# Third attention of a fused two-block transformer kernel: values in fp32r once a head and branch, a second transposed part, and the normalising pass on GpSimd

## The reference, cut to what matters

```python
o_c = jnp.einsum('bqghk,bkgd->bqghd', p_c, v_cmp)      # compressed keys, 31 of them
...
p_s = masked_softmax(ss, ...)                           # "selected" branch
o_s = jnp.einsum('bghqk,bgqkd->bqghd', p_s.astype(vs.dtype), vs)
...
p_w = masked_softmax(sw, mask_w)                        # "window" branch
o_w = jnp.einsum('bghqk,bkgd->bqghd', p_w.astype(vw.dtype), vw)
out = gc[..., 0:1] * o_c + gc[..., 1:2] * o_s + gc[..., 2:3] * o_w
```

## Time and profile before

| | |
|---|---|
| median of 3 runs | 1900.53 us (1900.32 to 1901.03) |
| the profiled execution: its own time, its span | 1901.72 us, 1899.9 us |
| mean granted clock of TensorE | 0.996 |
| TensorE busy | 1880.1 us (99% of the span) |
| VectorE, ScalarE, GpSimd busy | 879.0, 795.7, 952.2 us |
| nsa attention, first early-gate product to first merge product | 1277.47 to 1394.17 us |

### The profile page before, as it was taken

The page is one execution under the profiler, slowest core; times in us unless marked ns, Lnnn a source line. Parts: engine busy times, 40 slices in busy tenths (PEclk is TensorE's granted clock), DMA queues, the critical chain, the costliest instruction groups (busy, mean ns, idle before and its releaser), DMA issues.

```text
span 1899.9 us, 26936 instructions
## 1 busy us (share of the span) xinstructions
PE 1880.1 (99%) x9217; PEld 1572.9 (83%) x9217; DVE 879.0 (46%) x1814; ACT 795.7 (42%) x1412; POOL 952.2 (50%) x1236
## 2 busy tenths in 40 slices
PE   8999999999999999999999999999999999999999
PEld 6878888888888888888888888888888888888887
DVE  6867642222236675422222673696643354444200
ACT  6558742223233576422232353637652333323221
POOL 6640255554556642555555564552145555555553
PEclk9999999999999999999999999999999999999999
DMA  6330133232332212333323322221123323232332
GB/s 221 101 116 2 40 92 102 95 100 95 94 98 89 83 41 68 97 101 97 100 92 97 99 86 92 67 78 46 34 64 96 97 87 101 93 104 90 111 100 78
DMA packets 47438, 168.30 MB, mean 89 GB/s; under 512 B 5616, under 2 KB 5872, under 8 KB 47088
## 3 DMA queue, kind: packets, MB, share of 16 engines
q1 hardware_dynamic: 46368, 164.64, 27.0%
q10 hardware_dynamic: 976, 2.39, 0.5%
HBM read 164.13 MB, written 2.10 MB: 87 GB/s over the span
## 4 chain that ended last, share of the span: by engine, by line
PE 67%; POOL 14%; issue 14%; DVE 3%; ACT 1%; DMA 0%; POOLq 0%; SPq 0%; ACTq 0%; DVEq 0%
PE bank L611 19%; PE bank L613 19%; PE bank L612 19%; POOL WL L568 14%; PE bank L727 4%; PE bank L695 3%; PE bank L712 2%; PE bank L772 0%; DMA X<-x 0%; PE bank L777 0%; DVE KT L1436 0%; PE bank L666 0%; PE bank L724 0%; ACT PROB L1054 0%; DVE XL L1421 0%
## 5 line engine op out<-in xcount | busy, mean ns | idle before, releaser
L568 POOL TENSOR_TENSOR WL<-RAW,WH 128x256 fp32r<-128x256 f32 x1208 | 934.6, 806 | 919.1 <-ACT WH L990 918.8
L611 PE MATMUL bank<-XH,WH 128*128 128x512 f32 x1311 | 523.3, 399 | 2.0 <-DVE KMV L1758 1.0
L613 PE MATMUL bank<-XH,WL 128*128 128x512 f32 x1311 | 511.5, 390 | 0.0
L612 PE MATMUL bank<-XL,WH 128*128 128x512 f32 x1311 | 511.1, 390 | 0.0
L990 ACT ACTIVATE WH<-RAW 128x1024 fp32r<-128x1024 f32 x302 | 317.0, 1051 | 301.2 <-PE bank L613 297.5
L611 PEld LDWEIGHTS bank<-XH,WH 128*128 128x128 f32 x1311 | 246.7, 188 | 52.3 <-issue 2.6
L613 PEld LDWEIGHTS bank<-XH,WL 128*128 128x128 f32 x1311 | 246.5, 188 | 52.2
L612 PEld LDWEIGHTS bank<-XL,WH 128*128 128x128 f32 x1311 | 246.9, 188 | 49.1 <-issue 1.9
L611 PE MATMUL bank<-HH,WH 128*128 128x512 f32 x512 | 199.2, 389 | 0.0
L612 PE MATMUL bank<-HL,WH 128*128 128x512 f32 x512 | 199.2, 389 | 0.0
L613 PE MATMUL bank<-HH,WL 128*128 128x512 f32 x512 | 199.2, 389 | 0.0
(11 more groups left out here) (377 smaller groups left out, 2776.3 us busy)
## 6 DMA issues: line engine op xcount, KB each, us to landing
RAW<-stream SPq DMA_DIRECT2D x302, 512.0 KB, 3.5
out<-X SPq DMA_DIRECT2D x8, 256.0 KB, 4.6
X<-x SPq DMA_DIRECT2D x3, 512.0 KB, 7.4
MEM<-mem SPq DMA_DIRECT2D x1, 1024.0 KB, 10.7
W<-cmp_w ACTq DMA_DIRECT2D x1, 1024.0 KB, 4.6
KT<-KR ACTq DMA_DIRECT2D x1, 768.0 KB, 6.3
CT<-consts SPq DMA_DIRECT2D x1, 513.0 KB, 11.8
X<-x SPq DMA_DIRECT2D x2, 256.0 KB, 3.3
```

The costliest lines, as they stand in the source:

```text
L568: ins = pool.tensor_tensor(WL[:, slot, c], RAW[:, slot, c], WH[:, slot, c].bitcast(F32), ALU.subtract)
L611: pe.matmul(dst, lhs[0], rhs[0], start=start, stop=False)
L612: pe.matmul(dst, lhs[0], rhs[1], start=False, stop=False)
L613: return pe.matmul(dst, lhs[1], rhs[0], start=False, stop=stop)
```

## The change

1. Values (line 727) are made with fp32r operands: the value tile VN holds a high part (written by ScalarE) and a low part (VectorE) side by side as 128 stationary columns, and the transposed probabilities are kept as PTH (ScalarE's copy) and PTL (a new VectorE subtraction). The high and low halves of the output stand in the two halves of the bank's partitions and are added at a head's end by a second VectorE pass.
2. They are made once for a head and branch, of 10 matmuls of 512, 128, 256, 256 and 128 columns, each size twice; so the unit order becomes h, branch, b, and the burst stands in iterations i with i mod 4 = 2. TensorE then waits for `nsa_pt_lo` of the branch's fourth unit. The high part of the transposed units needs ScalarE at iteration j+5, the low part VectorE at iteration j+6.
3. Transposed units go round three banks, both branches and all heads write one output bank.
4. GpSimd does the normalising pass, one unit after another, and makes the pieces of the weight tiles' low parts between them.
5. Early gate products stand in every iteration with i mod 4 other than 2 (`GATE_AT`), three of them in iteration 0. Their outputs 0 to 5 begin in iterations 0, 8, 19, 29, 40 and 51, and are drained at the start of 8, 18, 29, 40, 50 and 61.

The core of the diff (tensor allocation is left out):

```diff
-PER_GATE = 10
+GATE_AT = [0, 0, 0] + [i for i in range(1, 64) if i % NT != 2]
...
-                     "nsa": (nsa_units(), ring(PROBW, ACC, SQ, TMP[:, 1:2, :]), ring(PT2, TMP[:, 0:1, :]))}
+                     "nsa": (nsa_units(), ring(TURN, ACC, SQ, TMP), None)}
...
-        TURNED = {name: [(o + 3) % RING, 4, 7][:3 if name == "mla" else 2] for name, o in AFTER.items()}
+        TURNED = {name: [(o + 3) % RING, 4] + {"mla": [7], "swa": [], "nsa": [6]}[name] for name, o in AFTER.items()}
...
+            for i, u in enumerate(units):
+                row, c = prob[i % len(prob)][:, u.keys], i % 8
+                pool.wait_ge(signal("nsa_summed"), i + 1)
+                pool.tensor_scalar(row, row, RS[:, c:c + 1], u.weight, ALU.mult, ALU.mult
+                                   ).then_inc(signal("nsa_prob"), 1)
+                for j in range(2 * EARLY_GATES):
+                    if 2 <= i - GATE_AT[KD * j] < 6:
+                        lo_piece(tile + j, (tile + j) % RING, i - GATE_AT[KD * j] - 2)
...
                     j = i - VALUE_LAG
-                    if 0 <= j:
+                    if 0 <= j and name in PAIRED and j % NT == NT - 1:
+                        u = units[j]
+                        pe.wait_ge(signal(name + "_pt_lo"), j + 1)
+                        bank = BANK[HEAD_OUT[name][u.head % 2]]
+                        if u.head and not u.stop:
+                            pe.wait_ge(signal(name + "_lo"), u.head)
+                        if name == "nsa" and u.stop:
+                            g, at = divmod(u.head, NH2 // NG)
+                            pe.wait_ge(signal("cmp_copied"), 2)
+                            pe.matmul(bank[0:HD, :], VC[:, at, HD * g:HD * g + HD], PCT[:, g, :], start=False, stop=False)
+                        order = [(j, 0), (j - 2, 1), (j, 1), (j, 2), (j, 3)]
+                        for last, kb in reversed(order) if u.stop else order:
+                            for part in (PTH, PTL):
+                                turned, to = turned_blocks(part, last, kb, bank)
+                                ins = pe.matmul(to, u.values[kb], turned, start=not u.stop and kb == 0 and part is PTH,
+                                                stop=u.stop and kb == 0 and part is PTL)
+                        ins.then_inc(signal(name + "_values"), 1)
...
+                    j = i - TURN_LAG - 1
+                    if name in PAIRED and 0 <= j < n:
+                        u = units[j]
+                        dve.wait_ge(signal(name + "_pt"), j + 1)
+                        dve.tensor_tensor(turned_part(PTL, j),
+                                          BANK[TURNED[name][j % len(TURNED[name])]][:, 0:u.nk].rearrange("p (a n) -> p a n", n=P),
+                                          turned_part(PTH, j).bitcast(F32), ALU.subtract
+                                          ).then_inc(signal(name + "_pt_lo"), 1)
-                    if 2 <= i < n + 2:
+                    if 2 <= i < n + 2 and name not in PAIRED:
...
+                        if name in PAIRED:
+                            own.then(dve.tensor_tensor(HEAD_LOW[0:HD, :], bank[0:HD, :], hi.bitcast(F32), ALU.subtract))
+                            dve.tensor_tensor(lo, bank[HD:P, :], HEAD_LOW[0:HD, :], ALU.add).then_inc(signal(name + "_lo"), 1)
...
+                act.activation(VN[:, b, :, :, 0:HD], BANK[o % RING][:, 0:2 * P].rearrange("p (r g n) -> p r g n", r=2, g=NG),
+                               ACT.Copy, scale=RCOL[:, b:b + 1]).then_inc(signal("v_hi"), 1)
...
-            late |= {PER_GATE * j + 9: early_gate(j) for j in range(2 * EARLY_GATES)}
+            late |= {GATE_AT[KD * j + KD - 1] + 1: early_gate(j) for j in range(2 * EARLY_GATES)}
```

More of the change, by code:

```diff
@@ L17 @@
+import itertools
 import math
@@ L58 @@
 TURN_LAG, VALUE_LAG = 5, 7
+PAIRED = ("nsa",)
 CHANNELS, LAST_V = 8, 23
@@ L464, in nsa_units @@
                 g = h // (NH2 // NG)
[L465 to L474, removed]
+                for br, b in itertools.product(range(2), range(NT)):
+                    nk = (b + 1) * P
+                    units.append(Unit(
+                        stacked(QN[:, h, blk(b)], KNH[:, br, g, 0:nk], KNL[:, br, g, 0:nk]), nk, TRI[:, S - nk:S],
+                        [VN[:, kb, br, g, :] for kb in range(b + 1)], 0, blk(b), start=False, stop=br == 1,
+                        weight=GATE[:, b, 3 * h + 1 + br:3 * h + 2 + br],
+                        head_end=yb_tile(h) if b == NT - 1 and br == 1 else None))
             return units
@@ L702, in attention @@
                         if j >= nt:
-                            pe.wait_ge(signal(name + "_pt"), j - nt + 1)
+                            pe.wait_ge(signal(name + ("_pt_lo" if name in PAIRED else "_pt")), j - nt + 1)
+                        elif name == "nsa" and j == 2:
+                            pe.wait_ge(signal("cmp_copied"), 1)
                         if rotated and j == 0:
@@ L716, in attention @@
                         u = units[j]
                         pe.wait_ge(signal(name + "_pt"), j + 1)
[L718 to L722, removed]
-                                g, at = divmod(u.head, NH2 // NG)
-                                pe.matmul(BANK[HEAD_OUT[u.head % 2]][:], VC[:, at, :], PCT[:, g, :], start=True,
-                                          stop=False)
+                        if u.head >= 2 and units[j - 1].head != u.head:
+                            pe.wait_ge(signal(name + "_lo"), u.head - 1)
@@ L726, in attention @@
                         for kb in range(u.nb):
-                            ins = pe.matmul(BANK[HEAD_OUT[u.head % 2]][:, u.out_cols], u.values[kb],
+                            ins = pe.matmul(BANK[HEAD_OUT[name][u.head % 2]][:, u.out_cols], u.values[kb],
                                             pt[j % len(pt)][:, blk(kb)],
@@ L947, in _ @@
                 for k in range(KD):
-                    late.setdefault(PER_GATE * j + 1 + k if j else max(k - 3, 0), []).append(early_gate(j, k))
+                    late.setdefault(GATE_AT[KD * j + k], []).append(early_gate(j, k))
             attention("nsa", meanwhile=late)
```

92 lines of the change are left out of this document (65 added, 27 removed).

## The result

| | before | changed |
|---|---|---|
| median (4 runs of each on one chip) | 1900.74 us (1900.32 to 1901.03) | 1916.37 us (1914.40 to 1917.96) |
| ratio, 95% interval | | 1.0083 (1.0071 to 1.0094) |
| nsa attention, first early-gate product to first merge product | 116.73 us | 133.74 us |

The account below looks back on a forecast made before the run. TensorE's matmuls were taken to bound the stage; -15.0 saved, -1.2 start wait, +6.3, +9.4, +6.1 and +5.0 new waits gave +10.6 us, a median of 1911.1 us from 1900.5. Range 1898 to 1918.

Parts of the forecast that it names:

- The bound: nsa attention stage: before the change it costs what TensorE's matmuls cost, busy 115.18 of 116.80 us.
- A: First burst and seven second branches: TensorE waits 0.70 us each for VectorE's last subtraction, 6.3 us together.
- B: First branches of heads 1 to 6: bursts wait 1.56 us each behind a head's end on VectorE, 9.4 us.
- C: Gate bank: gate products wait for VectorE's drain, and at iteration 8 GpSimd's pieces, 6.1 us together.
- D: End of the stage, last head: waits of 3.35 and 1.67 us with no gate product left, 5.0 us.
- What TensorE saves: Value matmuls in the stage: 35.5 us of fp32 rows become 16 bursts of 1.28, together 20.5, so -15.0 us.
- The rival of cheaper bursts: Value bursts: a 128-column matmul costs only its columns, 0.13 us less a burst, 1909.0 us; chance 0.08.
- the likeliest case: Whole kernel: the main forecast taken alone, 1906 to 1915 us, chance 0.50.
- costed at nothing: ScalarE's VN copies beside the first gate products (about 1.5 us uncovered) and GpSimd's normalising passes: no added time.
- Faster: Bursts: waits A and B don't arise, subtraction done before TensorE comes, 1890 us; chance 0.14.
- GpSimd late: GpSimd's normalising: four units take 4.5 us instead of 2.3, felt at start and tail, +2, 1913 us; chance 0.12.
- waits come at half the size: No-change rival: A and B at half size, waits 19.0 us in all, +2.8, 1903 us; chance 0.16.

Follow-up runs that it names:

- kernel 1: Changed kernel with VectorE's low-part subtraction moved ahead of the masking pass: 1910.03 us, ratio 1.0049.
- kernel 6: kernel 5 with two or three iterations free of gate products between one gate output and the next: 1896.93 us, ratio 0.9979.
- kernel 3: Changed kernel with dummy fp32r matmuls filling three of TensorE's longest waits (8, 8 and 6): 1914.33 us, ratio 1.0070.
- kernel 7: kernel 6 with the subtraction ahead of masking and GpSimd's pieces of the first and last tile two units earlier: 1893.62 us, ratio 0.9965.
- kernel 9: kernel 7 with normalising on VectorE and the weight tiles' low parts on GpSimd in one piece: 1898.48 us, ratio 0.9989.
- kernel 8: kernel 7 with the head's end one iteration earlier on ScalarE and VectorE: 1893.96 us, ratio 0.9964.
- kernel 2: Changed kernel with value bursts using the high part of the transposed probabilities twice, low part left out: 1903.50 us, ratio 1.0015.
- kernel 5: Changed kernel with the burst one iteration later (lag 8) and gate products in the other iterations: 1913.72 us, ratio 1.0069.
- kernel 10: Changed kernel, lag 7 kept, with only the gate outputs set apart by two or three iterations: 1914.40 us, ratio 1.0077.
- kernel 4: Changed kernel with normalising back on VectorE and GpSimd making only the weight tiles' low parts: 1927.38 us, ratio 1.0141.

## Why the prediction was right, and where it was not

**The bound.** Right. The stage was bound by TensorE, and the change made order the bound: with VectorE and ScalarE busy for 78 and 75 of 134 us, TensorE still waited for 22. Kernels 1 and 6 show that it is order, since they do the same work.

**The waits.** The term that decided the sign held nearly to the digit. Each wait with its 0.16, against the forecast:

| | forecast | measured |
|---|---|---|
| A, first burst and seven second branches | 6.3 | 5.4 (0.60 to 0.68 each, 0.35 for the first, 1.25 for the last) |
| B, behind six heads' ends | 9.4 | 9.4 (1.52 to 1.66 each) |
| C, second gate output; iterations 29, 40 | 6.1 (3.0; 1.35; 1.7) | 5.0 (2.18; 1.22; 1.62) |
| D, the end | 5.0 | 4.9 |
| together | 26.8 | 24.7 |

The 0.70 of A was 0.09 too long: from the end of the scores to the burst it took 1.29 us (1298.24 to 1299.53) and not 1.38, while TensorE's own 0.68 is right. In C the second gate output came 0.8 sooner than the 3.0 that I took, inside my bounds of 1.7 and 3.7.

**What TensorE saves.** This is the step that failed: -15.0. Work fell from 114.7 to 104.0 or 105.0 at full clock (kernels 3 and 7), so by 9.7 to 10.7. Where kernel 7 differs is found by adding up the distances from one start to the next, without waits, in its trace and in the one before (us):

| | before | kernel 7 |
|---|---|---|
| values | 31.2 | 23.2 |
| transposes | 17.8 | 14.9 |
| compressed branch | 6.9 | 8.0 |
| all else | 58.9 | 58.9 |

That is -9.7, and three terms make the difference to -15.0. First, the bursts took 1.40 to 1.50 us (1.44 to 1.49 in the changed kernel at full clock) in place of 1.28, 2.7 more in all: I had priced the sizes by pairs that follow a larger matmul, and missed the dear first matmul of a burst and the 0.05 of each that follows a smaller one. Second, the eight matmuls of the compressed branch take 1.00 us each (1299.53 to 1300.53) where all eight took 6.87 before, 0.86 each: 1.1. They now have an fp32r matmul behind them and 64 stationary columns instead of 128; which of the two costs it was not tried. Third, the value rows before took 31.2 and not 35.5. My 0.111 a row also holds what the change from fp32 to fp32r costs. As far as the rows show, that change did not go away with the values, since the transposes now stand ahead of it: of the 4.3 only 2.9 came off, at the transposes, and 1.4 did not. The rival of cheaper bursts pointed the wrong way. The Trainium skill's matmul rule (VectorE: DVE Perf Modes, "The TRN2 errata — SBUF-src ops pay a fixed extra latency per instruction") put a burst at an estimated 1.09 us; the measured one is a third longer, so the trace decides against the rule here.

**The clock.** Not in the prediction at all. TensorE's work was 108.2 us in place of 104.0 to 105.0, so the low clock cost 3.2 to 4.2. I had worked out waits of 3.0 and 3.35 us and treated them as idle time alone. The lower level can follow behind such a wait, and the matmuls after it then pay double.

**The sum.** Forecast +10.6 for the stage. Measured: work at full clock -9.7 to -10.7, waits +23.5 net of those before (forecast +25.6), clock +3.2 to +4.2, together the +17.0. The median moved by 15.6 against 10.6 forecast (1911.1). That is inside the range of 1898 to 1918 and above the likeliest case of 1906 to 1915. The top of the range was built from a late GpSimd, a C of 3.8 and a lost cover for VN, which did not come; that it took in 1916.4 was in part luck. TensorE was busy for 84% of the stage, far from the 98% that would have spoken against the forecast.

**GpSimd and costed at nothing.** Its passes took what the one-input estimate gave, by form in the changed stage (xcount, busy us, mean ns, idle before):

```profile
L633 POOL TENSOR_SCALAR SQ<-SQ,SM,GATE 128x512 f32<-128x512 f32 x6 | 4.6, 768 | 2.8 <-DVE SM L1577 2.8
```

That is 0.77 us against 0.72, and with 384 elements it took 662 ns against 0.62. No wait in mid-stage names GpSimd; the one of 2.02 us at iteration 8 does, as forecast in C. The covers held too, with one exception that I had not seen: a wait of 0.7 us for KCS (L968) early in the stage, which every kernel in the new form has (0.6 in kernel 9). The subtractions took 288 to 688 ns, as priced.

**The rivals.** Faster came true only for kernels 6 to 9, that is, with the order mended: its condition, waits A and B gone and under 12.4 us left, is met by kernel 6 with 6.5 us of waits, 8.1 with their 0.16 each. As the changed kernel stands it was out, for the reason given against it. That rival's sum had a slip: C and D as costed are 11.1 us and not 6, which gives 1895 in place of 1890. GpSimd late did not come; its four units are 3.8 us by that rival's own price, not 4.5. That waits come at half the size was wrong, too: B came in full.

## What to carry to other kernels

When work is taken off the engine that bounds a stage, write down for each point at which it will wait the fixed chain of the other engine from the last thing it feeds to the thing that it needs; mean loads say nothing, while this sum came out within 10% here. Mend the order at all such points together: the later burst and the spaced gate outputs gave some 2.7 and 2.0 us alone and 19.4 together, since a wait removed falls into the next one. Price a sequence of matmuls by a row in which the same sizes and types follow each other, its first one included, and where forecast waits are long, take slower matmuls behind some of them into the range.

## What the runs showed of the hardware

- TensorE's granted clock fell to 0.50 to 0.52 (1.2 of 2.4 GHz) behind some waits and not behind others, and the wait's length alone does not tell which. It fell behind 2.02 and 2.13 us in the changed kernel, 2.29 in kernel 1, 2.04 in kernel 2, 2.03 in kernel 5, 2.64 and 2.79 in kernel 10, and five waits of 1.75 to 1.99 in kernel 4; it did not behind 2.02 in kernel 1, 3.12 twice in kernel 5, 1.79 in kernel 10 and four of 1.75 to 2.15 in kernel 4, nor behind any of 1.0 to 1.5 us that came at full clock. In kernel 5 it also fell at the end of the stage, where no wait of the 28 us before was over 0.91 us, but several stood close together. Each fall came 0.7 to 1.6 us after TensorE had taken up work again. What decides between them stays open. With the waits filled (kernel 3) it stayed at 1.00.
- A matmul costs some 0.05 us more from start to start when it follows one with fewer columns: 256 after 128 takes 0.18 instead of 0.12, 512 after 128 takes 0.28 instead of 0.24. In the same bursts 128 after 512 or 256 takes 0.06, and the second of that pair 0.11. That weights or reads are the cause was not tried.
- GpSimd's pass over 128 x 512 fp32 with scalars took 768 ns, VectorE's masking and subtracting passes of that size out of PSUM 688. The same normalising pass on VectorE took 543 to 597 ns (by tile, in the trace before), so GpSimd needs 1.3 to 1.4 times as long, which costs nothing where the pass is not urgent.
